# A layer kernel's start: the first four weight units side by side, loaded and rounded in eighths

## The reference, cut to what matters

```python
z = jnp.einsum('btd,de->bte', x, w_in) + b_in      # x: 288 x 2048, w_in: 2048 x 6656
u = z[..., o3:o4]                                  # 1024 columns of it: the pooling branch's input
```

## Time and profile before

| what | value |
|---|---|
| median of 3 runs | 2361.52 us (2360.99 to 2361.74) |
| profiled execution, its own time | 2360.93 us |
| span of the profiled execution | 2359.1 us |
| mean granted TensorE clock | 0.994 |
| PE busy | 2323.9 us, 99% |
| first matmul | 8.03 us |
| unit 4's first matmul | 38.31 us |

### The profile page before, as it was taken

One profiled execution on the slowest core, in us unless ns is written; L12 is line 12 of the kernel. 1 busy time (PEld: TensorE's weight loads), 2 busy tenths in 40 slices (PEclk: granted clock), 3 DMA queues, 4 the chain that ended last, 5 costly groups with the idle time before them and its releaser, 6 DMA issues.

```text
span 2359.1 us, 47622 instructions
## 1 busy us (share of the span) xinstructions
PE 2323.9 (99%) x17515; PEld 2315.4 (98%) x17515; DVE 1405.9 (60%) x2337; ACT 880.4 (37%) x1079; POOL 1727.4 (73%) x711
## 2 busy tenths in 40 slices
PE   8999999999999999999999999999999999999996
PEld 8999999999999999999999999999999999999996
DVE  2875464465459973565555650657665777666656
ACT  4434453344544443333333333333333333333333
POOL 6875667777667777676767667787777777777775
PEclk9999999999999999999999999999999999999998
DMA  6553436654445555666666667866666666666552
GB/s 232 167 199 124 154 128 209 207 181 152 150 141 186 185 182 193 200 213 214 214 213 206 207 208 239 276 222 209 206 207 220 216 217 201 207 205 217 190 169 103
DMA packets 137081, 458.18 MB, mean 194 GB/s; under 512 B 13840, under 2 KB 32528, under 8 KB 136464
## 3 DMA queue, kind: packets, MB, share of 16 engines
q1 hardware_dynamic: 112752, 416.36, 54.7%
q10 hardware_dynamic: 24264, 40.93, 4.7%
HBM read 416.35 MB, written 43.28 MB: 195 GB/s over the span
## 4 chain that ended last, share of the span: by engine, by line
PE 98%; DVE 1%; ACT 0%; DMA 0%; issue 0%; SPq 0%; DVEq 0%; ACTq 0%
PE ps L1279 31%; PE ps L1280 31%; PE ps L1285 31%; PE ps L1565 1%; PE ps L1325 1%; PE ps L1511 0%; PE ps L1492 0%; PE ps L516 0%; DMA raw<-in_w_in 0%; PE ps L1417 0%; DVE R L480 0%; PE ps L1400 0%; PE ps L1428 0%; PE ps L1366 0%; ACT w_hi L627 0%
## 5 line engine op out<-in xcount | busy, mean ns | idle before, releaser
L600 POOL TENSOR_TENSOR w_lo<-raw,w_hi 128x1024 fp32r<-128x1024 f32 x700 | 1717.6, 2476 | 613.2 <-ACT w_hi L627 605.5
L627 ACT ACTIVATE w_hi<-raw 128x1024 fp32r<-128x1024 f32 x696 | 698.5, 1052 | 701.9 <-PE ps L1285 665.2
L1279 PE MATMUL ps<-a_hi,w_hi 128*128 128x288 f32 x3104 | 841.2, 297 | 5.4 <-issue 4.8
L1280 PE MATMUL ps<-a_lo,w_hi 128*128 128x288 f32 x3104 | 839.3, 297 | 0.0
L1279 PE MATMUL ps<-b_hi,w_hi 128*128 128x288 f32 (+1 forms) x2432 | 654.1, 296 | 0.4 <-ACT w_hi L627 0.4
L1280 PE MATMUL ps<-b_lo,w_hi 128*128 128x288 f32 (+1 forms) x2432 | 651.9, 294 | 0.0
L1279 PEld LDWEIGHTS ps<-a_hi,w_hi 128*128 128x128 f32 x3104 | 586.0, 189 | 7.9 <-issue 7.0
L1280 PEld LDWEIGHTS ps<-a_lo,w_hi 128*128 128x128 f32 x3104 | 585.9, 189 | 0.1
L1280 PEld LDWEIGHTS ps<-b_lo,w_hi 128*128 128x128 f32 x2432 | 458.2, 188 | 0.1
L1279 PEld LDWEIGHTS ps<-b_hi,w_hi 128*128 128x128 f32 x2432 | 456.7, 188 | 0.9 <-issue 0.8
L1285 PE MATMUL ps<-a_hi,w_lo 128*128 128x288 f32 x3104 | 440.9, 294 | 0.0
(11 more groups left out here) (195 smaller groups left out, 1204.9 us busy)
## 6 DMA issues: line engine op xcount, KB each, us to landing
raw<-in_peer_u SPq DMA_DIRECT2D x256, 512.0 KB, 4.4
raw<-in_peer_v SPq DMA_DIRECT2D x256, 512.0 KB, 4.1
raw<-in_w_in SPq DMA_DIRECT2D x104, 512.0 KB, 4.1
gelu_scratch<-F ACTq DMA_DIRECT2D x32, 576.0 KB, 5.6
gate_scratch<-g_stage ACTq DMA_DIRECT2D x36, 512.0 KB, 5.9
F<-gelu_scratch SPq DMA_DIRECT2D x32, 576.0 KB, 5.8
raw<-in_w_out SPq DMA_DIRECT2D x32, 512.0 KB, 3.8
raw<-in_w_query SPq DMA_DIRECT2D x32, 512.0 KB, 3.9
```

The source lines that it names most:

```text
L600: pool.tensor_tensor(wl[:, j, s], raw[:, j, s], wh[:, j, s].bitcast(F32), ALU.subtract).then_inc(lo_ready, 1)
L627: act.activation(wh[:, k, s], raw[:, k, s], ACT.Copy).then_inc(hi_ready, 1)
L1279: pe.matmul(out, w, mh(k), start=(n == 0), stop=False)
L1280: pe.matmul(out, w, ml(k), start=False, stop=False)
```

## The change

- Units 0 to 3 run side by side, each in its own PSUM bank. Units 2 and 3 get their own room: `RAW2` lies in `F`, and `WH2`, `WL2` in the space of `b_hi` and `b_lo`, all of it used by later stages.
- x and the four units come in eight pieces: two x tiles (288 KB, 128 x 576) and then an eighth of each unit (128 KB, 128 x 256). SP issues 40 loads where there were 8, all without a wait.
- ACT rounds 8 x pieces and 32 weight pieces. DVE makes all their low halves; POOL does nothing for these four units, and is let on with `lo_ready` set to 8.
- PE first runs seven matmuls of the 128 x 128 constant `ones` (float32, as are the norm's matmuls at L508) into bank 7, whose result nobody reads. Then, piece by piece, 24 matmuls each.
- Units 4 to 7 use banks 4 and 5 on PE, in code written out instead of a loop. SP loads units 4 and 5 as soon as DVE is through with the slot's pieces, then constants and state.
- The rounding of `g1` and `b1` moves behind the `u` units on ACT and DVE, because `b_hi` and `b_lo` are in use.

```diff
+            for q in range(PIECES):
+                x, s = slice(2 * q, 2 * q + 2), slice(W8 * q, W8 * q + W8)
+                sp.dma_start(R[:, x, :], xT[:, x, :]).then_inc(x_loaded[q], 16)
+                for u in range(FIRST_UNITS):
+                    sp.dma_start(first_w(u, raw, RAW2)[:, s], w_in[u, :, s]).then_inc(w_loaded[q][u], 16)
             sp.dma_start(vec[:, :], vecs).then_inc(vec_in, 16)
-            sp.wait_ge(lo_ready, 3)
-            stream(w_in, 2, 2, first=2)
+            for u in (4, 5):
+                for h in range(2):
+                    sp.wait_ge(w0_lo, FIRST_UNITS * (4 * h + 3) + u - 3)
+                    sp.dma_start(raw[:, u % 2, h * HU:h * HU + HU], w_in[u, :, h * HU:h * HU + HU])\
+                        .then_inc(loaded[2 * (u % 2) + h], 16)
             sp.dma_start(cst[:, :], consts).then_inc(consts_in, 16)
             sp.dma_start(SIN, stT).then_inc(state_in, 16)
-            stream(w_in, 4, 20, first=4)
+            stream(w_in, 6, 18, first=6)
...
# GpSimd
+            pool.wait_ge(w0_lo, FIRST_UNITS * PIECES)
+            pool.sem_inc(lo_ready, 2 * FIRST_UNITS)
+            with pool.Fori(FIRST_UNITS // 2, UNITS // 2) as i:
...
# ScalarE
+            for q in range(PIECES):
+                x, s = slice(2 * q, 2 * q + 2), slice(W8 * q, W8 * q + W8)
+                act.wait_ge(x_loaded[q], 16)
+                act.activation(ah[:, x, :], R[:, x, :], ACT.Copy).then_inc(x_hi, 1)
+                for u in range(FIRST_UNITS):
+                    act.wait_ge(w_loaded[q][u], 16)
+                    act.activation(first_w(u, wh, WH2)[:, s], first_w(u, raw, RAW2)[:, s], ACT.Copy)\
+                        .then_inc(w0_hi, 1)
+            act.wait_ge(w0_hi, FIRST_UNITS * PIECES)
+            act.sem_inc(hi_ready, 2 * FIRST_UNITS)
+            act.wait_ge(vec_in, 16)
...
+            act.wait_ge(outs_done, 2)
+            for h in range(2):
+                act.wait_ge(loaded[h], 16)
+                s = slice(h * HU, h * HU + HU)
+                act.activation(wh[:, 0, s], raw[:, 0, s], ACT.Copy).then_inc(hi_ready, 1)
+            for u in range(FIRST_UNITS):
+                ev_u(u, 0, bank=u)
+            units("u", 4, 4, lambda i, j: ev_u(i, j, bank=FIRST_UNITS + j))
...
# VectorE
+            for q in range(PIECES):
+                x, s = slice(2 * q, 2 * q + 2), slice(W8 * q, W8 * q + W8)
+                ve.wait_ge(x_hi, q + 1)
+                ve.tensor_tensor(al[:, x, :], R[:, x, :], ah[:, x, :].bitcast(F32), ALU.subtract).then_inc(x_lo, 1)
+                for u in range(FIRST_UNITS):
+                    ve.wait_ge(w0_hi, FIRST_UNITS * q + u + 1)
+                    ve.tensor_tensor(first_w(u, wl, WL2)[:, s], first_w(u, raw, RAW2)[:, s],
+                                     first_w(u, wh, WH2)[:, s].bitcast(F32), ALU.subtract).then_inc(w0_lo, 1)
...
# TensorE
+            pe.wait_ge(ones_set, 1)
+            for _ in range(7):
+                pe.matmul(OB[:, 0:P], ones[:, :], ones[:, :], start=True, stop=True)
+            def first_products(q, u, m, ready):
+                pe.wait_ge(ready, q + 1)
+                pe.wait_ge(w0_hi, FIRST_UNITS * q + u + 1)
+                for k in (2 * q, 2 * q + 1):
+                    pe.matmul(ps[:, u, 0:T], first_w(u, wh, WH2)[:, k * P:k * P + P], m[:, k, :],
+                              start=(k == 0 and m is ah), stop=False)
+            def first_low(q, u):
+                pe.wait_ge(w0_lo, FIRST_UNITS * q + u + 1)
+                for k in (2 * q, 2 * q + 1):
+                    last = pe.matmul(ps[:, u, 0:T], first_w(u, wl, WL2)[:, k * P:k * P + P], ah[:, k, :],
+                                     start=False, stop=(k == KT - 1))
+                return last
+            for q in range(PIECES - 1):
+                for u in range(FIRST_UNITS):
+                    first_products(q, u, ah, x_hi)
+                    if u:
+                        first_products(q, u - 1, al, x_lo)
+                first_products(q, FIRST_UNITS - 1, al, x_lo)
+                for u in range(FIRST_UNITS):
+                    first_low(q, u)
+            for u in range(FIRST_UNITS):
+                first_products(PIECES - 1, u, ah, x_hi)
+                first_products(PIECES - 1, u, al, x_lo)
+                first_low(PIECES - 1, u).then_inc(outs_done, 1)
+            for n in range(4):
+                if n >= 2:
+                    pe.wait_ge(ev_act, n + 3)
+                product(FIRST_UNITS + n % 2, n % 2, FULL, a_op(ah), a_op(al), UNIT0["u"] + FIRST_UNITS + n)
```

More of the change, by code:

```diff
@@ L76 @@
 TG = TOKS * 8
+FIRST_UNITS = 4
+PIECES = 8
+W8 = KT * P // PIECES
 ROT = (0, 1, 3, 4)
@@ L204, in layer @@
         GG, o_front = carve(0, 32, T)
+        RAW2, _ = carve(0, 2, KT * P)
+        WH2, WL2 = (t.rearrange("p k t -> p (k t)")[:, 0:2 * KT * P].rearrange("p (u n) -> p u n", u=2)
+                    for t in (bh, bl))
         UP, o = carve(o_front, 8, 16 + SEQ)
@@ L288, in layer @@
         ev_act, ev_dve = sem("evicted_by_act"), sem("evicted_by_dve")
-        x_loaded = [sem(f"x_loaded_{n}") for n in range(4)]
+        x_loaded = [sem(f"x_loaded_{n}") for n in range(8)]
+        w_loaded = [[sem(f"first_w_loaded_{q}_{u}") for u in range(FIRST_UNITS)] for q in range(PIECES)]
+        w0_hi, w0_lo = sem("first_w_hi"), sem("first_w_lo")
         vec_in = sem("vec_in")
@@ L324, in layer, with first_w @@
         u_rows, state_set = sem("u_rows_gathered"), sem("pool_state_set")
+        def first_w(u, slots, more):
+            return slots[:, u, :] if u < 2 else more[:, u - 2, :]
         block = ctx.enter_context(nc.Block())
@@ L534, in stream @@
                         load(src[first + 2 * i + j], u0, i, j)
[L537 to L542, removed]
-            sp.dma_start(vec[:, :], vecs).then_inc(vec_in, 16)
-            sp.wait_ge(lo_ready, 3)
-            stream(w_in, 2, 2, first=2)
+            for q in range(PIECES):
[3 more added lines that the diff above has]
+                    sp.dma_start(first_w(u, raw, RAW2)[:, s], w_in[u, :, s]).then_inc(w_loaded[q][u], 16)
+            sp.dma_start(vec[:, :], vecs).then_inc(vec_in, 16)
+            for u in (4, 5):
[3 more added lines that the diff above has]
+                        .then_inc(loaded[2 * (u % 2) + h], 16)
             sp.dma_start(cst[:, :], consts).then_inc(consts_in, 16)
             sp.dma_start(SIN, stT).then_inc(state_in, 16)
-            stream(w_in, 4, 20, first=4)
+            stream(w_in, 6, 18, first=6)
             sp.wait_ge(d_split, PG)
@@ L605, in lower @@
                     lower_half(j, h, 4 * i + 2 * j + h + 1)
-            for n, (h, j) in enumerate(((0, 0), (0, 1), (1, 0), (1, 1))):
-                lower_half(j, h, n + 1)
-            with pool.Fori(1, UNITS // 2) as i:
+            pool.wait_ge(w0_lo, FIRST_UNITS * PIECES)
+            pool.sem_inc(lo_ready, 2 * FIRST_UNITS)
+            with pool.Fori(FIRST_UNITS // 2, UNITS // 2) as i:
                 for j in range(2):
@@ L624, in hi @@
                 for h in range(2):
-                    act.wait_ge(loaded[2 * k + h], 16 * (UNIT0[phase] // 2 + (j + 1) // 2 + 1) + i * 8)
+                    act.wait_ge(loaded[2 * k + h], 16 * ((UNIT0[phase] - FIRST_UNITS) // 2 + (j + 1) // 2 + 1) + i * 8)
                     s = slice(h * HU, h * HU + HU)
@@ L641, in _ @@
             act.sem_inc(g_stored, 65)
[L642 to L650, removed]
@@ new lines, in _, with ev_u @@
+            act.wait_ge(w0_hi, FIRST_UNITS * PIECES)
+            act.sem_inc(hi_ready, 2 * FIRST_UNITS)
+            act.wait_ge(vec_in, 16)
+            def ev_u(i, j, bank=None):
+                bank = j if bank is None else bank
+                wait_out("u", i + j)
+                bias = V("b_in")[:, bass.ds(i + j, 1)]
+                act.activation(UP[:, bass.ds(i + j, 1), 16:16 + SEQ], ps[:, bank:bank + 1, 0:SEQ], ACT.Identity,
+                               bias=bias)
+                act.activation(US[:, bass.ds(i + j, 1), :, 16:20].rearrange("p a b s -> p (a b) s"),
+                               ps[:, bank, SEQ:T].rearrange("p (b s) -> p b s", b=DB),
+                               ACT.Identity, bias=bias).then_inc(ev_act, 1)
@@ L653, in _ @@
             act.activation(bh[:, :, T + 1:T + 2], V("b1").unsqueeze(2), ACT.Copy).then_inc(gb_hi, 1)
[L655 to L666, removed]
             act.wait_ge(ev_act, 8)
@@ L671, in _ @@
                            US[:, :, :, 16:20].rearrange("p a b s -> p (a b) s"), ACT.Copy).then_inc(u_rows, 1)
-            act.wait_ge(x_lo, 4)
+            act.wait_ge(x_lo, 8)
             def ev_kv(i, j):
@@ L881, in _ @@
             ve.wait_ge(ev_act, 8)
+            for n, name in enumerate(("g1", "b1")):
+                ve.wait_ge(gb_hi, n + 1)
+                ve.tensor_tensor(bl[:, :, T + n:T + n + 1], V(name).unsqueeze(2),
+                                 bh[:, :, T + n:T + n + 1].bitcast(F32), ALU.subtract).then_inc(gb_lo, 1)
             ve.wait_ge(consts_in, 16)
@@ L1308, in _ @@
```

(4 more changed lines are left out.)

## The result

The changed kernel takes 2414.61 us (median of 5 runs, 2412.13 to 2415.69), the kernel before 2361.52 (2360.85 to 2361.74 in the same comparison): ratio 1.0226, 95% interval 1.0215 to 1.0237. It is 53 us slower, where 7 us faster was forecast.

The account below looks back on a forecast made before the run. TensorE, busy 99% of the span, was taken as the bound. Of 12.75 us lost at the start, 5.4 + 0.2 + 0 + 0 = 5.6 would remain, a gain of 7.1: 2354.4 us, range 2351.2 to 2359.2.

Parts of the forecast that it names:

- E: Any TensorE stop at unit 4 or later, behind the new start: taken as 0; some 2 us if loads came 3 us late.
- the rival on the other side: At the start, the 40 small loads are the bound, each costing far more than its bytes: kernel at 2373 us; chance 0.07.
- waits in a queue: 160 waits on TensorE in the start: costed at nothing, up to 4.8 us if the queue of weights did not run ahead.
- S: Time of the first product's matmul at the new start, after x and the first weights are loaded and rounded: 5.4 us.
- G: Gaps on TensorE while the start's pipe fills: 0.2 us, up to 1.0 if each station is at its slow end.
- Stations: SP issue, transfer, ACT and DVE in the start: 2.3 to 2.4 us a piece each, below TensorE's 3.20.
- C: Slow-clock loss in the start: 0 if the constant matmuls lift the clock before real work, else 2.5 us.
- T: Time at which unit 4 begins on TensorE, behind the new start: 31.2 us.
- The later drop: TensorE's half-speed stretch after 193 us, costing 3.1 us: change taken as 0; its vanishing gives 2351.3, chance 0.10.

## Why the prediction was wrong

**The step that failed** is the one behind E: "The rest of the kernel is paced by TensorE and moves with it. One thing does not: the clock." A second thing does not: the place of code. The change makes TensorE's program 465 instructions longer ahead of the peer_v loop; that moves the loop from 42 behind a block boundary to 5 ahead of one, and every one of the six jumps back costs 10 us, 60 in all. My list of what else could go wrong held nothing of the kind: the rival on the other side (small loads as the bound) had the sign and no part of the mechanism. Changes of the code's length in the diff, units 4 to 7 written out and 192 matmuls with their waits, I had costed as waits in a queue only. The instruction transfers were on the page of before, 43 of them, and I read past the row.

The Trainium skill's page "Runtime: NRT & Kernel Launch", section Instruction fetch mechanics, says that TensorE holds 128 KiB of instructions, refilled in 16 KiB blocks. The transfers here are of that size, and by this figure 8 blocks would just fit. The trace points to what takes their room: each pass moves nine blocks, so with the loop's 8 one more is fetched, which may be the one behind the loop, fetched ahead. Which block it is no run shows. The same section says that a taken branch whose target lies outside a window of two pages waits for a fetch. The waits agree with this where 8 blocks are touched; where 7 are touched the jump reaches as far back and fetches nothing, so the window here is wider than two.

**The rest of the sum held within half a microsecond.** With the loop's place mended the kernel takes 2354.32 us, and the sum said 2354.4; unit 4 starts at 31.64, and the sum said 31.2. That closeness is partly luck, since S was 0.4 too high and G 0.9 too low:

- S was 5.4; measured 4.88 (4.84 to 4.97 in the others). ACT could start on x at 3.75, sooner than the estimate of 4.1.
- G was 0.2. With the clock full from 5.28 unit 4 starts at 31.64: 31.64 - 4.97 - 25.56 = 1.1 for gaps and what is left of the slow clock. All of it lies in the first piece, from 4.97 to 9.26 us where 3.20 was due; one wait there, 0.34 us, is for a weight piece, and of the rest only part is the slow clock until 5.28. From the second piece on the 160 waits cost nothing: 24 matmuls took 3.2 us.
- Stations: VectorE's 256 columns took 0.418 us (0.42 said), ACT's 0.40, an issue 0.43, a piece's issues 2.4 us (2.4 said). The loads did not hold TensorE up; the rival of the small loads is refuted.
- C was 0. In the profiled run of the changed kernel it was not: the pace was 0.24 us a matmul until 9.6 us, in spite of seven constants from 1.38 to 4.4. In four other traces with the same start the clock was full from 5.28, 5.73, 7.52 and 7.59, with nine constants from 4.69, in the two without any from 8.88 and 9.90. So the constants lift it earlier in most traces, but when it comes varied by 4 us.
- E was 0 at unit 4, and is: in the changed kernel GpSimd's first low half of unit 4 began at 31.84 and ended by T + 1.5, and the units ran on.
- The later drop (half speed from 190.5 us; the first group of small matmuls took 1.97 us and the second 3.44) lasted 6.8 us as before; its place moved with the work, and its length was 3.4 to 10.2 us in the traces.

## What to carry to other kernels

Before an edit that lengthens or shortens straight code, count instructions up to each long loop behind it and see how many 16 KB blocks each touches; where the blocks begin, a stop inside the loop of one trace tells. On TensorE a loop of 7 blocks ran without a stop and one of 8 paid 8 to 10 us at every jump back. The sign in a profile is instruction transfers that keep coming during a loop, with idle time "issue" just behind its jump. An edit of some microseconds at the start can be judged only when such a loop has been put back: here the same start reads as 53 us lost or 7 us gained.

## What the runs showed of the hardware

- Four instructions in some 11,600 decide over 62 us (2354.32, and 2416.15 in one run).
- A loop that touches 8 blocks of instructions moves nine in each pass (54 transfers more in six passes), one that touches 7 moves none.
- A semaphore increment on TensorE's queue costs 0.15 us in a row of 120, three times the 0.051 us of its own record.
- With identical code before it, the clock came to full speed between 5.28 and 9.60 us (five traces), and the half-speed stretch near 190 us was 3.4 or 6.8 us long: a spread of a few microseconds between traces, in a kernel whose gain is 7.
